# Mean of squares of four RMS norms: quartered rows on TensorE against tokens on the rows

## The reference, cut to what matters

```python
def rms_norm(x):
    xf = x.astype(jnp.float32)
    return (xf * lax.rsqrt(jnp.mean(xf * xf, axis=-1, keepdims=True) + EPS)).astype(x.dtype)

h = rms_norm(x) * P['norm_mix'][layer] * (1 + sc1) + sh1
...
x = x + g1 * y
h = rms_norm(x) * P['norm_ffn'][layer] * (1 + sc2) + sh2
x = x + g2 * conv_ffn(h, ...)
```

## Time and profile before

| | us |
|---|---|
| median of 3 runs | 2042.51 |
| lowest, highest | 2038.42, 2044.99 |
| profiled execution, its own time | 2045.66 |
| span of the profiled execution | 2043.9 |
| PE busy | 1942.5 (95%) |
| DVE busy | 1252.4 (61%) |
| ACT busy | 810.4 (40%) |
| mean granted TensorE clock | 0.973 |

### The profile page before, as it was taken

How to read it: one execution, slowest core, us unless ns; L and a number is a source line. 1 busy time by engine, 2 the same in 40 slices (tenths; PEclk the granted TensorE clock), 3 DMA queues, 4 the chain that set the end, 5 groups by cost and what they waited for, 6 DMA issues and landing times.

```text
span 2043.9 us, 32999 instructions
## 1 busy us (share of the span) xinstructions
PE 1942.5 (95%) x13393; PEld 1848.3 (90%) x13393; DVE 1252.4 (61%) x1891; ACT 810.4 (40%) x1349; POOL 150.3 (7%) x127
## 2 busy tenths in 40 slices
PE   6998889999998989999999989999998999999999
PEld 3998779999987979999999989966688999999999
DVE  4655843566765777777887786656635553453553
ACT  3545533222435245414314335555524551342441
POOL 0011620000000000000000013511100000000000
PEclk8999989999998989999999999999998999999999
DMA  7221002344330423343343332200011222222222
GB/s 297 83 71 46 12 11 83 124 144 134 113 114 12 134 73 113 124 144 123 114 154 113 114 105 65 63 3 1 1 42 42 83 72 73 79 68 79 72 65 79
DMA packets 57062, 175.96 MB, mean 86 GB/s; under 512 B 7552, under 2 KB 9472, under 8 KB 56832
## 3 DMA queue, kind: packets, MB, share of 16 engines
q1 hardware_dynamic: 55152, 172.20, 26.2%
q10 hardware_dynamic: 1808, 2.36, 0.3%
HBM read 170.07 MB, written 4.47 MB: 85 GB/s over the span
## 4 chain that ended last, share of the span: by engine, by line
PE 79%; issue 8%; DVE 8%; ACT 2%; POOL 1%; DMA 1%; SPq 0%; POOLq 0%; ACTq 0%; DVEq 0%
PE ps L378 71%; DVE t_sb L723 1%; PE ps L1205 1%; DVE h_lo L733 1%; POOL hf L2102 1%; PE ps L806 1%; PE ps L1192 1%; DVE w_lo L369 1%; PE ps L1543 1%; ACT w_hi L361 1%; PE ps L1554 1%; DMA modw<-in_w_modA 1%; PE ps L1208 1%; DVE x L821 1%; PE ps L1148 0%
## 5 line engine op out<-in xcount | busy, mean ns | idle before, releaser
L378 PE MATMUL ps<-h_hi,w_hi 128*128 128x322 f32 x2768 | 645.5, 315 | 19.1 <-ACT h_hi L761 10.4
L378 PE MATMUL ps<-h_lo,w_hi 128*128 128x322 f32 x2768 | 641.2, 313 | 4.5 <-DVE h_lo L733 3.7
L378 PE MATMUL ps<-h_hi,w_lo 128*128 128x322 f32 x2768 | 640.6, 313 | 0.0
L369 DVE TENSOR_TENSOR w_lo<-raw,w_hi 128x1024 fp32r<-128x1024 f32 (+1 forms) x221 | 270.3, 1223 | 507.9 <-ACT w_hi L361 507.8
L361 ACT ACTIVATE w_hi<-raw 128x1024 fp32r<-128x1024 f32 (+1 forms) x221 | 230.7, 1044 | 742.5 <-PE ps L378 738.4
L378 PEld LDWEIGHTS ps<-h_hi,w_hi 128*128 128x128 f32 x2768 | 469.2, 191 | 23.8 <-issue 17.0
L378 PEld LDWEIGHTS ps<-h_lo,w_hi 128*128 128x128 f32 x2768 | 471.1, 191 | 8.9 <-DVE h_lo L733 8.1
L378 PEld LDWEIGHTS ps<-h_hi,w_lo 128*128 128x128 f32 x2768 | 471.4, 191 | 0.0
L378 PE MATMUL ps<-hid_hi,w_hi 128*128 128x322 f32 x704 | 161.5, 311 | 1.6 <-DVE x L821 1.5
L378 PE MATMUL ps<-hid_hi,w_lo 128*128 128x322 f32 x704 | 162.1, 311 | 0.0
L378 PE MATMUL ps<-hid_lo,w_hi 128*128 128x322 f32 x704 | 161.7, 311 | 0.0
(11 more groups left out here) (276 smaller groups left out, 2044.6 us busy)
## 6 DMA issues: line engine op xcount, KB each, us to landing
raw<-in_ffn_up SPq DMA_DIRECT2D x88, 512.0 KB, 3.6
raw<-in_hyb_in SPq DMA_DIRECT2D x49, 512.0 KB, 3.7
mrawB<-in_w_modB SPq DMA_DIRECT2D x48, 512.0 KB, 4.3
mrawA<-in_w_modB SPq DMA_DIRECT2D x64, 256.0 KB, 2.8
raw<-in_ffn_down SPq DMA_DIRECT2D x32, 448.0 KB, 3.3
raw<-in_hyb_out SPq DMA_DIRECT2D x16, 512.0 KB, 3.9
raw<-in_ffn_down SPq DMA_DIRECT2D x16, 512.0 KB, 3.6
modw<-in_w_modA SPq DMA_DIRECT2D x12, 512.0 KB, 12.6
```

The lines of the kernel that those rows point to most:

```text
L369: dve.tensor_tensor(w_lo[:, i % 2, 0:n], raw[:, b % RAW, 0:n], w_hi[:, i % 2, 0:n].bitcast(F32), SUB).then_inc(S("w_lo"), 1)
L378: last = pe.matmul(pj(f)[:, hh, :], w[:, i % 2, k * 128:(k + 1) * 128], v[:, k, hh * HALF:(hh + 1) * HALF], start=(k == 0 and n == 0), sto ...
```

## The change

In the wide norms, only the first six tiles are added on DVE. The squares of the seventh stay in `sq[:, 0, :]`. PE takes 128-token chunks of `ssq`, of the seventh tile's squares and of the eighth's as the stationary side, with one column of ones as the moving side, into three sets of five columns. DVE sums the three sets (a new reduce, 128 x 5 from 128 x 15), ACT takes the root and DVE the reciprocal of 128 x 5 values, and PE spreads as in the narrow norm. The two hooks move by one unit: `pe_mod_sum` stands ahead of unit 7, `dve_mod` behind the residual of unit 7.

```diff
-            SQ0[p] = sum(KT - 1 if q in WIDE else KT for q in NORMS[:NORMS.index(p)])
+            SQ0[p] = sum(KT - 2 if q in WIDE else KT for q in NORMS[:NORMS.index(p)])
...
-        MS = flat[:, 2048 + 640:2048 + 640 + NCH]
+        MS3 = flat[:, 2048 + 640:2048 + 640 + 3 * NCH].rearrange("p (n c) -> p n c", n=3)
+        MS = MS3[:, 0, :]
...
-            pe.wait_ge(S("sq_add"), SQ0[name] + KT - 1)
-            for q in range(4):
-                pe.matmul(MSQ[32 * q:32 * q + 32, :], ones[:, 0:32], ssq[:, QC * q:QC * q + QC], start=True, stop=False)
-            for q in range(4):
-                if q == 0:
+            pe.wait_ge(S("sq_add"), SQ0[name] + KT - 2)
+            for c in range(NCH):
+                pe.matmul(MS3[:, 0, c:c + 1], ssq[:, chunk(c)], ones[:, 0:1], start=True, stop=True)
+            pe.wait_ge(S("sq"), KT * i + KT - 1)
+            for c in range(NCH):
+                pe.matmul(MS3[:, 1, c:c + 1], sq[:, 0, chunk(c)], ones[:, 0:1], start=True, stop=True)
+            for c in range(NCH):
+                if c == 0:
                     pe.wait_ge(S("sq_a"), WIDE.index(name) + 1)
-                elif q == 2:
+                if c == 2:
                     pe.wait_ge(S("sq"), KT * (i + 1))
-                last = pe.matmul(MSQ[32 * q:32 * q + 32, :], ones[:, 0:32], sq[:, 1, QC * q:QC * q + QC], start=False, stop=True)
+                last = pe.matmul(MS3[:, 2, c:c + 1], sq[:, 1, chunk(c)], ones[:, 0:1], start=True, stop=True)
             last.then_inc(S("ms"), 1)
...
-            if name in WIDE:
-                for q, c0, c1 in ((0, 0, QC), (1, QC, 2 * QC), (2, 2 * QC, 3 * QC), (3, 3 * QC, 512), (3, 512, TOK)):
-                    last = pe.matmul(flat[:, 2048 + c0:2048 + c1], ident[:, 32 * q:32 * q + 1].to_broadcast([128, 128]),
-                                     rq[:, c0 - QC * q:c1 - QC * q], start=True, stop=True)
-                last.then_inc(S("tp_full"), 1)
-                return
...
-                act.wait_ge(S("ms"), STEP0[name] + 1)
-                act.activation(rq, MSQ, ACT.Sqrt, bias=eps, scale=1.0 / D_MODEL).then_inc(S("root"), 1)
+                act.wait_ge(S("ms_sum"), WIDE.index(name) + 1)
+                act.activation(rs[:, 0, :], rs[:, 1, :], ACT.Sqrt, bias=eps, scale=1.0 / D_MODEL).then_inc(S("root"), 1)
...
-                dve.wait_ge(S("root"), STEP0[name] + 1)
-                dve.reciprocal(rq, rq).then_inc(S("rstd"), 1)
-                return
+                dve.wait_ge(S("ms"), STEP0[name] + 1)
+                dve.tensor_reduce(rs[:, 1, :], MS3.rearrange("p n c -> p c n"), AX.X, ADD).then_inc(S("ms_sum"), 1)
...
-                else:
-                    dve_add_square(dve, norm, r - 1)
...
-                if r == 6:
+                if r == 7:
                     pe_mod_sum(pe, 2, 8)
...
-            for k in range(KT - 1):
+            for k in range(KT - 2):
                 dve_add_square(dve, "norm00", k)
...
-            dve_out_stage(dve, stages["wo_ret"], gate(0, 2), "norm01", None, {6: lambda: dve_mod(dve, "modC", MA // 4 + 2)})
+            dve_out_stage(dve, stages["wo_ret"], gate(0, 2), "norm01", None, {7: lambda: dve_mod(dve, "modC", MA // 4 + 2)})
...
-                              {6: lambda: dve_mod(dve, "modD", MA // 4 + 3)} if n == 2 else {})
+                              {7: lambda: dve_mod(dve, "modD", MA // 4 + 3)} if n == 2 else {})
...
-                         {6: lambda: pe_mod_sum(pe, 8, 20)} if n == 2 else None)
+                         {7: lambda: pe_mod_sum(pe, 8, 20)} if n == 2 else None)
```

More of the change, by code:

```diff
@@ L616, in build @@
             STEP0[p] = NORMS.index(p)
-            SQ0[p] = sum(KT - 1 if q in WIDE else KT for q in NORMS[:NORMS.index(p)])
+            SQ0[p] = sum(KT - 2 if q in WIDE else KT for q in NORMS[:NORMS.index(p)])
             TN0[p] = sum(KT for q in NORMS[:NORMS.index(p)])
-        QC = TOK // 4
-        MSQ, rq = B6[:, 0:QC], hf2[:, 0, 0:QC]
         def half(hh):
@@ L720, in scaled @@
                 for (c0, c1), at in GROUPS:
-                    p0 = 2048 + (c0 if wide else at)
-                    by = flat[:, p0:p0 + c1 - c0]
+                    by = flat[:, 2048 + at:2048 + at + c1 - c0]
                     ins = dve.scalar_tensor_tensor(tn[:, d % 2, c0:c1], src[:, k, c0:c1], scale(k, int(at > 0)), by, MUL, MUL)
```

## The result

| | before | after |
|---|---|---|
| median of 15 runs each | 2042.45 | 2046.40 |
| lowest to highest | 2038.14 to 2047.42 | 2043.11 to 2049.82 |
| profiled execution, its own time | 2045.66 | 2044.9 |
| profiled execution, its span | 2043.9 | 2043.1 |

The ratio of after to before is 1.0020, with a 95% interval of 1.0011 to 1.0029. That is 4.0 us slower (2.2 to 5.9): within the 0.3% that the prediction called no change, but clearly slower. Against the median the prediction had 0 to +1. One execution of the kernel with only the hooks moved took 2139 us at a mean granted clock of 0.84; the ratio given for it leaves that one out, and its median without it is 2040.19.

A forecast was written before the change was run, and what follows sets the result against it. TensorE, 79% of the chain, and serial joints between stages were taken as the bound. At full clock, norm00 +2.5, norm01 -2.3, norm10 0 and norm11 -1.0 gave -0.8 us on 2045.66, so 2045; range 2038.5 to 2052.

The forecast's parts named there:

- What bounds the kernel: Whole kernel: TensorE is 79% of the chain; joints between stages are serial; norm00's chain runs through PE without a gap.
- Pace and price of the sums: Each wide norm: PE sets the pace, 30 records at 0.115 us, sums done 3.5 us after the last unit.
- Reduce, root, reciprocal: Between sums and spread in each wide norm: 0.8 us with handovers, where it was 1.65.
- The spread at 1.46: Last PE step before the apply: ten 128-column records at full clock, making a norm 5.8 us in all.
- norm00 at +2.5: First wide norm, where PE's own time counts: the longer sums cost 2.5 us at full clock.
- The clock rival: One-column sums count as idleness, so the clock falls: +5.5 us together, 2051; chance 0.35.
- DVE's lateness: norm01: the removed add and moved dve_mod made DVE late, but PE's 3.5 us hide this; only 0.1 us gained.
- The hooks: pe_mod_sum one unit later costs the same on PE; dve_mod fits in the some 2 us before the reduce.
- The number: Whole kernel: 2045 in the profiled execution's own time, chance 0.5; against the median 0 to +1.
- The two small rivals: Two alternatives: norm00 without cost, 2042.4, chance 0.1; sums ready with the squares, 2038, chance 0.05.
- That norm00 costs nothing: norm00 waits for modulation weights or its units 12 to 15 close up: the 2.5 falls away, 2042.4; chance 0.1.
- That the sums would be done with the squares at 1.8 us: All four norms: PE's records go faster than 0.115 us, each norm gains 1.7 more, total 2038; chance 0.05.

The follow-up runs named there:

- The 96-column kernel: The changed kernel with 96 columns of ones instead of one as the moving side in all fifteen matmuls, sets in three PSUM banks; 2038.82, ratio 0.9975.

## Why the prediction was right and wrong

- **What bounds the kernel.** Right. PE's own time ahead of unit 15 is the path in norm00, and the joints are serial.
- **Pace and price of the sums.** Right at full clock: 0.112 us a record, 3.3 to 3.6 us in all with 96 columns. In the kernel after, where the clock fell in the third set, they took 3.6 to 4.0 between stages and 5.5 in norm00.
- **Reduce, root, reciprocal.** Taken at 0.8, measured 0.8 to 0.95. The reduce itself is 0.17 against 0.19. The root on five columns is 0.30 when it reads SBUF, where 0.27 was taken from PSUM.
- **The spread at 1.46.** This is the step that failed, with the clock behind it. It was 2.50 in all three norms of the kernel after, and the last sums were slow too: 7.1 to 7.3 us a norm, not 5.8. The 96-column kernel, at a clock of 1.00, spreads in 1.40 and has 5.6 to 5.7 us in norm01 and norm11.
- **norm00 at +2.5.** The term was mis-sized by the clock as well: +6.8 from unit 11 on in the profiled execution, about +5 by the medians of the run that changes norm00 alone. With 96 columns it is +2.0, since units 12 and 13 overlap more than I took.
- **The clock rival.** It is what happened, and it had 0.35. That the form of the matmuls decides, and neither PE's busy share nor the wait behind the sums, is shown by the edit from 1 to 96 columns; the three PSUM banks that came with it were not tried alone. Its time was put at 2051, some 5.5 above the profiled execution of before; measured were 4.0 above the median. The parts were sized otherwise than they came: norm00 was to lose 1.5 us by the clock and lost 4.7 (14.5 against 9.8 with 96 columns), since the clock stayed low for 10 us and not for 3 us of work. Norm01 lost 1.4 and norm11 1.7, near the 1.6. The edit from 1 to 96 columns is worth 7.6 us by the medians, 9 by the ratios.
- **The Trainium skill**, "TensorE: Matmul & The Clock Gate", Part 4: PE-mode transpose, says of transposes that the full clock does not engage for them, since they do not count as busy in the same way. The windows show something like it for matmuls of one column behind full loads: busy 1.00, clock 0.50. No run here isolates transposes.
- **DVE's lateness.** Held to be hidden behind PE's 3.5 us, and so it was in norm01 of the kernel after. In norm10 it is not when the attention's weights land late; that case was not in the prediction.
- **The hooks.** Costed at nothing, and this was wrong too: `pe_mod_sum` was said to cost the same one unit later, but in its old place ahead of norm10 it held PE idle for 2.15 us in both profiled executions that have it there (the kernel before and the run that changes norm00 alone), and in none of the other eight. In the kernel before, moving the hooks alone gained 3 us. So the change carried a gain that the sum did not have, and the new form of the sums probably lost more than the 4.0 us by which the kernel got slower.
- **The number.** The median's +4.0 is outside the 0 to +1 that was argued for it and inside the stated range. That the profiled execution came out at 2044.9 is luck: +5.4 us in the norms and their stages stood against 5.3 us in stretches that the change does not touch.
- **The two small rivals.** That norm00 costs nothing fell: it cost about 5 us. That the sums would be done with the squares at 1.8 us fell too: even with ten matmuls they took 2.7.

## What to carry to other kernels

A matmul's price on an engine that is the path has two parts: the time of its load and stream, and what it does to the clock of the work behind it. Before small sums are moved to TensorE as full 128-column loads with one streamed column, ask what clock the matmuls behind them need. Where the load sets the pace anyway, streaming more columns can be free and can keep the clock; it did not in norm10 of one run, where PE had first stood idle for 1.7 us. And a form that fits a joint where PE is idle (norm01, norm11) can be wrong at a place where PE is the path (norm00): undo it there alone. Last, a step moved along with a change has a price of its own: look for the wait that it causes in its old place, and run the move by itself.

## What the runs showed that was not expected

- Ten records of 128-column loads with 96 streamed columns took 1.11 to 1.13 us, and with one streamed column 1.12.
- The clock fell to 0.50 while PE and PEld both showed 1.00 busy with one-column matmuls; with 96 columns it stayed at 1.00 in the same place.
- At a clock of 0.50 the spacing of these loads is 0.213 us, 1.9 times the 0.112 at full clock: the loads slow down with the clock.
- An add of 644 columns on DVE takes 0.82 us (L649), but the two at norm10 took 2.34 together (1.34 and 0.90) in two of the three runs of the column form with seven tiles added, each while a GpSimd operation on two tensors was under way. No run tried it without them, so the cause is not shown.
